# Gate matmuls of a recurrent unit in f16 terms, later in the slot

## The reference

```python
u = _causal_conv(xa, conv_w, conv_b)
ub = u.reshape(bsz, s, LRU_BLOCKS, LRU_BLOCK)
r = jax.nn.sigmoid(jnp.einsum('bshi,hij->bshj', ub, w_r).reshape(bsz, s, w) + b_r)
i = jax.nn.sigmoid(jnp.einsum('bshi,hij->bshj', ub, w_i).reshape(bsz, s, w) + b_i)
log_a = -LRU_C * r.astype(f32) * jax.nn.softplus(-lam.astype(f32))
a = jnp.exp(log_a)
beta = jnp.sqrt(-jnp.expm1(2.0 * log_a))
_, h = lax.associative_scan(_combine, (a, beta * (i * u).astype(f32)), axis=1)
return h.astype(xa.dtype) * jax.nn.silu(ga)
```

## Time and profile before

| | |
|---|---|
| Median of 3 runs | 1997.5 us |
| Lowest and highest | 1995.81 and 1997.83 us |
| The profiled execution | 1992.77 us |
| Its span, first to last instruction | 1991.1 us |
| Mean granted clock of TensorE | 0.996 |
| TensorE busy | 1937.7 us, 97% |
| VectorE, ScalarE, GpSimd busy | 60%, 49%, 24% |

### The profile page before, as it was taken

How to read it: one execution, slowest core, us unless ns; L and a number is a source line. 1 busy time by engine, 2 the same in 40 slices (tenths; PEclk the granted TensorE clock), 3 DMA queues, 4 the chain that set the end, 5 groups by cost and what they waited for, 6 DMA issues and landing times.

```text
span 1991.1 us, 27991 instructions
## 1 busy us (share of the span) xinstructions
PE 1937.7 (97%) x11102; PEld 1057.7 (53%) x11102; DVE 1189.5 (60%) x1477; ACT 969.8 (49%) x1793; POOL 473.0 (24%) x298
## 2 busy tenths in 40 slices
PE   6999999999999999999979999999999999999998
PEld 3446665455456665544444466654554566655443
DVE  6676766377436766544366768663773366765434
ACT  5774333356325666543347643433653356665323
POOL 0213443133212222111002134522331222221110
PEclk9999999999999999999989999999999999999999
DMA  5224222343334443234132242123433343432441
GB/s 185 85 85 128 64 85 64 117 117 88 104 101 124 120 117 112 85 127 143 54 108 80 69 131 82 64 85 101 117 101 104 104 131 98 115 107 85 154 139 42
DMA packets 205519, 205.14 MB, mean 103 GB/s; under 512 B 29504, under 2 KB 196423, under 8 KB 205383
## 3 DMA queue, kind: packets, MB, share of 16 engines
q1 hardware_dynamic: 205383, 203.29, 33.3%
HBM read 176.00 MB, written 4.19 MB: 91 GB/s over the span
## 4 chain that ended last, share of the span: by engine, by line
PE 42%; DVE 5%; ACT 2%; issue 1%; DVEq 0%; ACTq 0%
PE PS L477 40%; DVE wsp L1028 1%; DVE X L1031 1%; ACT X L888 1%; DVE M L1028 1%; DVE Y L1028 0%; PE PS L665 0%; DVE small L1031 0%; DVE small L1121 0%; PE PS L743 0%; ACT wsp L770 0%; PE PS L711 0%; ACT X L773 0%; PE PS L583 0%; DVE Y L1031 0%
## 5 line engine op out<-in xcount | busy, mean ns | idle before, releaser
L477 PE MATMUL PS<-hT,wsp 128*128 128x512 f16 x4896 | 1082.3, 379 | 0.0
L477 PEld LDWEIGHTS PS<-hT,wsp 128*128 128x128 f16 x4896 | 475.9, 98 | 561.4 <-issue 11.2
L1028 DVE SCALAR_TENSOR_TENSOR wsp<-stage,wsp 128x2048 f16<-128x2048 f32 x150 | 384.9, 2566 | 199.5 <-ACT wsp L770 198.3
L477 PE MATMUL PS<-ys,wsp 128*128 128x512 f16 x1536 | 340.0, 379 | 0.0
L770 ACT ACTIVATE wsp<-stage 128x2048 f16<-128x2048 f32 x150 | 285.3, 1902 | 90.7 <-PE PS L477 86.8
L477 PEld LDWEIGHTS PS<-ys,wsp 128*128 128x128 f16 x1536 | 149.6, 98 | 177.8 <-issue 3.0
L477 PE MATMUL PS<-wsp,hT 128*128 128x256 f16 x1728 | 194.5, 273 | 0.0
L477 PEld LDWEIGHTS PS<-wsp,hT 128*128 128x128 f16 x1728 | 168.7, 98 | 23.6 <-issue 2.3
L1345 POOL TENSOR_TENSOR M<-M,T 128x512 f32<-128x512 f32 x48 | 69.6, 1456 | 342.8 <-DVE T L1028 342.8
L1345 POOL TENSOR_TENSOR X<-X,K 128x1024 f32<-128x1024 f32 x26 | 62.9, 2421 | 349.2 <-DMA X<-X 349.2
L773 ACT ACTIVATE X<-PS 128x512 f32<-128x512 f32 x120 | 68.6, 593 | 123.7 <-PE PS L477 90.9
(11 more groups left out here) (186 smaller groups left out, 2036.5 us busy)
## 6 DMA issues: line engine op xcount, KB each, us to landing
stage<-w_in SPq DMA_DIRECT2D x122, 1024.0 KB, 5.1
stage<-w_branch SPq DMA_DIRECT2D x32, 1024.0 KB, 5.0
X<-X SPq DMA_DIRECT2D x120, 128.0 KB, 2.3
stage<-w_out SPq DMA_DIRECT2D x8, 1024.0 KB, 5.7
out<-xres SPq DMA_DIRECT2D x8, 512.0 KB, 2.6
Y<-Y SPq DMA_DIRECT2D x24, 128.0 KB, 2.3
xres<-x SPq DMA_DIRECT2D x4, 512.0 KB, 4.9
Y<-T SPq DMA_DIRECT2D x16, 128.0 KB, 2.5
```

Source lines behind the costliest of these rows:

```text
L477: return pe.matmul(o, a, b, start=start, stop=stop, skip_group_check=True)
L1028: return dve.scalar_tensor_tensor(out=o, in0=a, scalar=c, in1=b, op0=op0, op1=op1)
```

## The change

The gate weights and the convolution's output get a high half and a remainder in f16 (`wbd16` in a free part of Y, `conv16` in a free part of X), and each gate is three f16 matmuls that add up in PSUM instead of one in f32. The weights are scaled by 64, so the gate activations scale by a 64th of the old factor. ScalarE makes the high halves and VectorE the remainder of the weights in `middle` of slot 1; in `middle` of each "ga" slot ScalarE copies the high halves of the convolution, and GpSimd subtracts for the remainders. The gates move from step 2 to step 6 of their slot. TensorE now waits for `wbd_lo` and `conv_lo`, and no longer for the DMAs or for VectorE's convolution itself.

```diff
--- before.py
+++ after.py
@@ -100,7 +100,7 @@
 CONV_SLOTS = [p for p in range(NP) if PANELS[p][0] in ("xa", "conv")]
 
 
-GATES_AT = 2
+GATES_AT = 6
 SCAN_SLOT = {(SLOT[("vc", 0)] if _j == 3 else SLOT[("ga", _j)] + 2): _j for _j in range(4)}
 LOCAL_OUT_AT = 8
 
@@ -253,6 +253,9 @@
         gC = [Y[:, 5120 + 1024 * b:6144 + 1024 * b].rearrange("p (u s) -> p u s", u=2) for b in range(2)]
 
         wbd = Y[:, 3072:5120].rearrange("p (t r n) -> p t r n", t=8, r=2)
+        wbd16 = Y[:, 5120:7168].bitcast(F16).rearrange("p (h t r n) -> p h t r n", h=2, t=8, r=2)
+        wbd16_flat = Y[:, 5120:7168].bitcast(F16).rearrange("p (h n) -> p h n", h=2)
+        conv16 = X[:, 4096:5120].bitcast(F16).rearrange("p (h u s) -> p h u s", h=2, u=2)
 
         dtw = Y[:, 2048:2176].rearrange("p (k n) -> p k n", k=KT)
         dtws = Y[:, 2176:2304].bitcast(F16).rearrange("p (h k n) -> p h k n", h=2, k=KT)
@@ -304,7 +307,7 @@
                  "load0", "load1", "hi_done", "lo_done", "tile_done", "act_free", "dve_free", "gate_ready",
                  "act_chain", "dve_chain", "pool_chain",
                  "xn_T", "h_hi", "h_lo", "dt_raw", "sp_in", "sp_exp", "dta_ready", "cs_done", "cs_ready", "dec_ready", "lru_par",
-                 "conv_first", "lru_gates", "lru_a", "lru_v", "lru_w", "lru_a2", "lru_vv", "lru_ww", "lru_beta", "lru_bw",
+                 "conv_first", "wbd_hi", "wbd_lo", "conv_hi", "conv_lo", "lru_gates", "lru_a", "lru_v", "lru_w", "lru_a2", "lru_vv", "lru_ww", "lru_beta", "lru_bw",
                  "lru_y", "y_hi", "y_lo", "conv_tanh", "conv_silu", "xt_done", "xt_read",
                  "rope_dma", "rope_sin", "rope_done", "rope_hi", "rope_lo", "rope_stack",
                  "ssd_tri", "ssd_x", "ssd_g", "ssd_exp", "ssd_mt", "ssd_y", "ssd_read", "ssd_out", "ssd_st", "ssd_ss", "ssd_norm", "ssd_T",
@@ -685,14 +688,18 @@
                     for u in range(2):
                         t = 2 * PANELS[p - 1][1] + u
                         if t == 0:
-                            pe.wait_ge(s["wbd_in"], 64)
+                            pe.wait_ge(s["wbd_lo"], 1)
                             pe.wait_ge(s["dec_ready"], 1)
                         if t >= 2:
                             pe.wait_ge(s["lru_w"], t - 1)
                             pe.wait_ge(s["lru_v"], t - 1)
-                        pe.wait_ge(s["dve_free"], dve_frees(2 * SLOT[("xa", t // 2)] + u))
-                        mm(PS[:, 4 + 2 * u, :], wbd[:, t, 0, :], cbuf[:, u, :], True, True)
-                        mm(PS[:, 5 + 2 * u, :], wbd[:, t, 1, :], cbuf[:, u, :], True, True).then_inc(s["lru_gates"], 1)
+                        pe.wait_ge(s["conv_lo"], t + 1)
+                        for r in range(2):
+                            o = PS[:, 4 + 2 * u + r, :]
+                            mm(o, wbd16[:, 0, t, r, :], conv16[:, 0, u, :], True, False)
+                            mm(o, wbd16[:, 0, t, r, :], conv16[:, 1, u, :], False, False)
+                            last = mm(o, wbd16[:, 1, t, r, :], conv16[:, 0, u, :], False, True)
+                        last.then_inc(s["lru_gates"], 1)
 
             def middle(p):
                 if p in TURN_OF:
@@ -864,14 +871,14 @@
                     for u in range(2):
                         t = 2 * j + u
                         act.wait_ge(s["lru_gates"], t + 1)
-                        link(act.activation(rbuf[:, u, :], PS[:, 4 + 2 * u], ACT.Tanh, scale=0.5, bias=halfA[:, A_BR + t:A_BR + t + 1]))
+                        link(act.activation(rbuf[:, u, :], PS[:, 4 + 2 * u], ACT.Tanh, scale=0.5 * IWS, bias=halfA[:, A_BR + t:A_BR + t + 1]))
                         act.activation(abuf[:, u, :], rbuf[:, u, :], ACT.Exp, scale=nsp4[:, t:t + 1], bias=nsp4[:, t:t + 1])\
                             .then_inc(s["lru_a"], 1)
                         act.activation(vbuf[:, u, :], rbuf[:, u, :], ACT.Tanh, scale=sp4[:, t:t + 1], bias=sp4[:, t:t + 1])\
                             .then_inc(s["lru_v"], 1)
                         act.activation(rbuf[:, u, :], rbuf[:, u, :], ACT.Exp, scale=nsp8[:, t:t + 1], bias=nsp8[:, t:t + 1])\
                             .then_inc(s["lru_a2"], 1)
-                        act.activation(wbuf[:, u, :], PS[:, 5 + 2 * u], ACT.Tanh, scale=0.5, bias=halfA[:, A_BI + t:A_BI + t + 1])\
+                        act.activation(wbuf[:, u, :], PS[:, 5 + 2 * u], ACT.Tanh, scale=0.5 * IWS, bias=halfA[:, A_BI + t:A_BI + t + 1])\
                             .then_inc(s["lru_w"], 1)
                 if p > 0 and PANELS[p - 1][0] == "conv":
                     for u in range(2):
@@ -924,6 +931,16 @@
                         copy(dPT[:, e, 0:nk], PS[:, 4 + 2 * e, 0:nk]).then_inc(s["df_Tr"], 1)
 
             def middle(p):
+                if p == 1:
+                    act.wait_ge(s["wbd_in"], 64)
+                    copy(wbd16_flat[:, 0], wbd.rearrange("p t r n -> p (t r n)"), WS).then_inc(s["wbd_hi"], 1)
+                if PANELS[p][0] == "ga":
+                    for u in range(2):
+                        t = 2 * PANELS[p][1] + u
+                        act.wait_ge(s["dve_free"], dve_frees(2 * (p - 1) + u))
+                        if t >= 2:
+                            act.wait_ge(s["lru_gates"], t - 1)
+                        copy(conv16[:, 0, u, :], cbuf[:, u, :]).then_inc(s["conv_hi"], 1)
                 if p - 1 in DIFF_END:
                     h2 = DIFF_END[p - 1]
                     for u in range(2):
@@ -1270,6 +1287,10 @@
                     tt(z[g][:, c, :], z[g][:, c, :], yf, ALU.mult).then_inc(s["ssd_y"], 1)
 
             def middle(p):
+                if p == 1:
+                    dve.wait_ge(s["wbd_hi"], 1)
+                    stt(wbd16_flat[:, 1], wbd.rearrange("p t r n -> p (t r n)"), WS, wbd16_flat[:, 0], ALU.mult, ALU.subtract)\
+                        .then_inc(s["wbd_lo"], 1)
                 if p in SSD_END:
                     g = SSD_END[p]
                     for t in range(4):
@@ -1413,6 +1434,11 @@
                 if p > 0 and PANELS[p - 1][0] in ROTATED:
                     rope(p - 1)
                     rotated_lo(p - 1)
+                if PANELS[p][0] == "ga":
+                    for u in range(2):
+                        t = 2 * PANELS[p][1] + u
+                        pool.wait_ge(s["conv_hi"], t + 1)
+                        tt(conv16[:, 1, u, :], cbuf[:, u, :], conv16[:, 0, u, :], ALU.subtract).then_inc(s["conv_lo"], 1)
                 if p in SCAN_SLOT:
                     for u in range(2):
                         t = 2 * SCAN_SLOT[p] + u
```

## The result

| | before | changed |
|---|---|---|
| Median of 6 runs each, us | 1996.65 | 2004.51 |
| Lowest and highest | 1994.48 to 1997.83 | 2002.09 to 2006.07 |
| Ratio, 95% interval | | 1.0044 [1.0033, 1.0054] |
| The profiled execution, its span | 1992.77, 1991.1 | 2002.09, 2000.2 |
| Mean granted clock in it | 0.996 | 0.995 |

The change makes the kernel slower, by 7.9 us in the medians. The forecast was 6.4.

A forecast was written before the change was run, and what follows sets the result against it. TensorE, 97% busy, bounds the kernel; the ScalarE-VectorE chain beside it has no slack. Per layer, waits of 6.6 less savings of 4 x 0.85 give +3.2 us; 1997.5 + 6.4 = 2003.9 us, range 1998 to 2011.

The forecast's parts named there:

- Gate matmuls, 0.85 us saved per slot: On TensorE, 12 f16 matmuls take 2.59 us instead of 3.44, in 8 slots, 6.8 us in all.
- Weights to f16 in slot 1: ScalarE copies from 46.02 to 47.92, VectorE's remainder runs from 47.98 to 50.27; nothing taken for the DMA wait.
- Slot 2: Its gates start at 51.46 after a TensorE wait of 1.08 us; first tanh at 53.01.
- The y product's 0.78 us goes away: VectorE's second y product drops from 1.47 to 0.69 us, as GpSimd's y remainder comes after the convolution copies.
- A cycle of 25.14 us: From tanh to next tanh through ScalarE, VectorE and GpSimd in slots 2 to 8, where TensorE needs 23.31 us.
- +3.2 us per layer: Slot 8 ends at 135.94 instead of 132.75 us; +6.4 us over two layers.
- They shift as a block: nothing given back, nothing added: Stages behind slot 8 follow TensorE's panels, so they neither recover nor add time.
- The clock stays at 1.00 in the waits of slots 2 to 8: TensorE's waits of 1.1 to 1.9 us lie below a 2.38 us gap at full clock: no loss.
- Rival 1: The recurrent chain stays off the path, TensorE never waits: 6.8 us faster, 1990.7 us; 10%.
- Rival 2: VectorE's 0.78 us stays through another GpSimd collision: cycle 25.92 us, +4.7, 2008.6 us; 17%.
- Rival 3: TensorE's clock falls to 0.50 in the waits of slots 2 to 8: +10 us, 2014 us; 6%.
- Rival 4: Waits of 0.85 us per slot, from shorter handovers, cancel the gate saving: 1997.5 us; 9%.

The follow-up runs named there:

- tenth run: The changed kernel once more, unaltered: 2003.61 us, ratio 1.0042 to the kernel before.
- ninth run: The eighth run, with ScalarE's weight copy and slot 1's convolution copies early too, GpSimd there waiting for VectorE's evacuation: 1989.63 us, ratio 0.9973.
- first run: The kernel before with its f32 gates moved from step 2 to step 6, nothing else: 1994.51 us, ratio 1.0001.
- third run: The changed kernel with the gates at step 9 instead of 6: 2000.95 us, ratio 1.0027.
- fifth run: The changed kernel without GpSimd's subtractions, the convolution's low half being zeros and TensorE waiting for ScalarE's copies: 2004.14 us, ratio 1.0043.
- second run: The changed kernel with its gates back at step 2: 2021.18 us, ratio 1.0138.
- eighth run: The changed kernel with ScalarE's copies early in slots 3, 5, 7 and GpSimd's subtractions held until VectorE's second y product: 1990.65 us, ratio 0.9979.
- sixth run: The changed kernel with ScalarE's convolution copies moved ahead of its y copies, where it waits for the scans: 2007.19 us, ratio 1.0056.

## Why the prediction was right in kind and short in size

The sign, the place and the mechanism were right; the size was 6.4 us, measured are 7.9 in the first comparison and 8.6 in the tenth run's. Its points in turn:

- **Gate matmuls, 0.85 us saved per slot:** right, 2.59 us for 12, and the ninth run gets all of it.
- **The later step costs only start time:** right (first run). The third run adds what the prediction didn't say: only slot 2 gains by a later step.
- **Weights to f16 in slot 1:** right, and the wait for their DMAs costs nothing there. ScalarE's copy followed its activation without a wait (45.78, 1.89 us) and VectorE's remainder took 2.29.
- **Slot 2:** the gates were to start 10.54 us behind the small matmuls on Y and K of slot 1 (51.46 - 40.92), and started 10.49 behind (51.16 - 40.67). The wait, 1.08, is 0.87 + 0.16 = 1.03.
- **The y product's 0.78 us goes away:** right, 0.69 measured; the fifth run shows it come back when GpSimd isn't parked.
- **A cycle of 25.14 us:** 25.11. The waits of 1.80 (1.64 + 0.16) were forecast at 1.83. The subtractions took 2.27 for two, so 1.14 each, against 1.16.
- **+3.2 us per layer:** +3.07 and +3.08. Per layer 1.03 + 3 x 1.80 - 3.40 = 3.03 by the rows.
- **Its path was too simple.** It went through GpSimd's subtraction alone. ScalarE's own queue, with the copies, has a cycle of 24.88 us, only 0.23 less, so with the subtraction taken away the queue sets the cycle (fifth run). The sum didn't compare the two; that it took the longer one was in part luck.
- **"They shift as a block: nothing given back, nothing added":** this is the step that failed, and why the size came out short. Added were 0.24 to 0.52 us in each attention stage, where a transfer on the instruction queue now falls on four copies, by inference its cause. The clock dips are in both kernels. The 6.15 us of the slots and these 0.6 leave 1.1 us of the 7.9 open, and 1.9 of the 8.6; 0.3 to 1.2 of that may lie behind the attention stage of layer 2, as in the other versions with f16 gates, and its cause stays open.
- **The clock stays at 1.00 in the waits of slots 2 to 8:** right for the change. "A gap of 2.38 us lies in a stretch at 1.00" was no safe bound: it is the idle time of the weight loads, and the same gap is a wait of 1.92 in TensorE's own row, the measure by which the second run's waits are 2.09. There the clock fell, and in the first run it fell at that very place, after 1.93.
- **Rival 1 (chain off the path)** is false for the change, and true for runs 8 and 9. The prediction asked for a cycle of 23.3 or less; these have 23.84, and the lead of 1.45 us in slot 4 suffices for the cycles that are left. **Rival 2** is false; the fifth run shows what it describes, the y product back at 1.47 us, though there the chain runs through ScalarE. **Rival 3** is false here, true at step 2. **Rival 4** is false: the hand-over estimated at 0.17 is 0.16 (first subtraction from 74.98 by 1.14 to 76.12, gates at 76.28).

## What to carry to other kernels

When matmuls are made cheaper by preparing their operands on other engines, add up the cycle of the engine that prepares them, queue and all; if that cycle is longer than TensorE's, a later start of the matmuls helps once and never again, and a cut in TensorE's work comes through only in part. Look for the idle time in the preparing engine's queue and move the work there, but then find out which two-input operations of VectorE the GpSimd work will land on, and hold it back with a wait where it would. In this kernel the early copies alone cost 2.7 us more than the change; with the hold on GpSimd, and the weights early too, +7.9 us turned into -5.4. The hold without the early copies wasn't run.

And when a later stage moves although nothing in it was edited, look at the DMA queues as well, the one for instructions included: in this kernel the added matmuls went with a shift, by some 5 us, of the moment at which a piece of the program is loaded.

## What the runs showed of the hardware that was not expected

- TensorE's clock fell to 0.50 after repeated waits of 2.09 us (second run) and after others of 1.93 (first run), 2.15 (ninth run, layer 1) and 2.17 (third and fifth run), and stayed at 1.00 after others of 2.15 (eighth run, and the ninth in layer 2), 2.28 (changed kernel, layer 1) and 2.48 (second run, attention stage). The length of the wait alone, within 1.9 to 2.5 us, doesn't tell.
- With the same 2.09 us waits, layer 1 ran three gate groups at full speed and the fourth slow; layer 2 ran all four slow.
- VectorE's scan (128x512, two inputs in SBUF) is held by GpSimd like the two-input operations: 1.22 us became 2.17 (sixth run). So is a cast of 128x64 with only one input there: 0.20 us became 0.86 (ninth run).
- Four copies that SyncE issues in 2.47 or 2.48 us took 2.92 to 3.67 wherever a 16 KB transfer on the instruction queue started 0.8 to 1.5 us behind the first, in 18 layers of 18; in the 6 where it started 5.4 to 6.1 us behind, none was slow.
